# Sparse heads in pairs inside the common loop, output products between a turn and its values, a third place for the last output chunk

## The chip, the cores and the metric

The kernel runs on one core of one Trainium2 chip. The metric is device time in microseconds (us); smaller is better. TensorE (PE) multiplies, VectorE (DVE) and ScalarE (ACT) work on tiles, GpSimd (POOL) takes some elementwise work, SyncE (SP) only starts DMAs. Each engine works through its own queue in order and waits there for semaphores.

## The reference, cut to what matters

The program is two transformer layers and one further block on 256 tokens of width 1024, in float32. The change lies in the first layer's mixer. Its output is a product of 16 heads (1024 columns) with a 1024x1024 matrix. Eight heads (NSA) have a compressed, a selected and a window branch; with 256 tokens the last two are full causal attention on two sets of keys. Eight heads (DSA, "sparse") attend to the 64 best tokens by an index score, with keys and values made from a latent of 128 numbers per token:

```python
ckv = rms_norm(kv_lat, kv_norm)
q_lat = jnp.einsum('bshd,rhd->bshr', q, w_uk)
_, idx = lax.top_k(isc, topk)                 # isc: index score, topk = 64
logits = jnp.einsum('bqhr,bqkr->bhqk', qlb, c_sel) * scale + bias
p = masked_softmax(logits, (dist >= 0)[:, None])
o_lat = jnp.einsum('bhqk,bqkr->bqhr', p, c_sel)
o = jnp.einsum('bqhr,rhd->bqhd', o_lat, w_uv)
```

The kernel does not gather: it adds -1e30 to the logits of tokens that are not chosen. Then come the output product, a residual with layer norm, and the MLP.

## The kernel before, in words

Weights stream from memory in 1 MB chunks into a ring of four slots. Each chunk is split into a rounded high part (ACT, `round_weights`, L493) and a remainder (DVE, `lower_weights`, L499). The split parts have two places in SBUF for chunks 0 to 11 and three from chunk 12 (the first MLP chunk, MLP0) on; a place can be rewritten when the chunk before it there is "used" by PE. Chunks 8 to 11 (EV_OUT to EV_OUT + 3) hold the output matrix. A split product is three matmuls (L505 to L507).

Attention works in units of 384 columns (the two query tiles see 128 and 256 keys). Units 0 to 15 are NSA heads by branch, units 16 to 23 (DSA0 to DSA0 + 7) the sparse heads. For each unit: PE makes logits; DVE scales them, adds the bias and takes two maxima (`unit_logits_vector`, L1056 to L1061); ACT takes exponentials (L1067); DVE makes the coefficient (L1328, L1330, for sparse units L1325); POOL scales by it (L1074); PE turns the result with three transposes (L1082); ACT copies it out of PSUM (`pT`, L1089); PE multiplies with the values. There are four slots (NB) for units. In units 2 to 14 DVE also finds the chosen tokens in eight rounds (L1311, L1316); their mask is made at unit 14.

The first loop takes NSA units in pairs, d = 0 to 7: two units' logits lie in the two halves of the rows of the PE array, and their values in the two halves of its columns (L1046, L1048, L1175, L1177). It also makes the sparse queries in the latent space (`ql`, L1205). After it sparse units go one by one over the full array: logits against the latent (L1038, L1039), values (L1236, L1237), an ACT copy `olat`, and a product with `w_uv` (L1247). Chunk 8 and chunk 9 of the output product (`out_step`, 24 matmuls each) lie after pair 6's values and in step 3; chunks 10 and 11 come in a tail of 48 matmuls (`out_tail`), after DVE has finished head pair 7. Then `norm_vector` and `norm_scalar` run, and the MLP starts.

PSUM has eight banks. `Banks.take` (L184) pops the first free bank and makes PE wait until whatever was there last has been read; a bank taken with hold stays out of the list until `give`. The output product holds four banks from `out_begin` on. A finished head pair's bank is given back at once, but whoever takes it next waits for DVE's `head_out_vector` (L1097), which comes after ACT's `head_out_scalar` (L1093).

Of the kernel before, what the change touches and what calls it, by code (L numbers as in the profile page):

```python
# [291 lines left out]
def program(nc, I, out):  # L292
    ctx = ExitStack()
    with ctx:
# [69 lines left out]
        qlatT = mem.take("qlatT", 8, SEQ, at=iq_at)  # L364
# [16 lines left out]
        ukT = mem.take("ukT", 4, P)  # L381
# [10 lines left out]
        olat = mem.take("olat", 2, SEQ, at=ln_at + 4 * UC)  # L392
# [615 lines left out]
        def ev_gpsimd(e):  # L1008
# [16 lines left out]
            e.wait_ge(*landed.at("bias", 2))  # L1025
# [8 lines left out]

        def unit_logits_tensor(e, u, lhs, rhs):

            b = ps.take(e, ("unit", u), vec, "z", u)
            e.matmul(b[:, 0:P], lhs(0), rhs(tok(0)), start=True, stop=True)  # L1038
            e.matmul(b[:, P:UC], lhs(1), rhs(ALL), start=True, stop=True).then_inc(*pe.up("logits", u))  # L1039
# [67 lines left out]
        def out_multiply(e, tag, c, src, t, first, last):  # L1107
            w_ = weights(c)
            for kk, (h_, l_) in enumerate(src):
# [42 lines left out]
        def sparse_logits_tensor(e, h):  # L1152
            unit_logits_tensor(e, DSA0 + h, lambda t: qlatT[:, h, tok(t)], lambda c: ckvT[:, c])

        def two_logits_tensor(e, d):
            h, branch = NSA[2 * d]
            kk = BRANCH[branch][0]
            pair_logits_tensor(e, 2 * d, lambda r, t: qT[HALVES[r], h // 2, tok(t)], lambda r, c: kk[HALVES[r], h // 4, c])

        def two_values_tensor(e, d):  # L1160
            h, branch = NSA[2 * d]
            g, c0, i = h // 4, BRANCH[branch][1], h // 2
            v_ = lambda t: v_sw[:, t, c0 + g * HALF:c0 + (g + 1) * HALF]
            if branch == 0:
                ps.take(e, ("heads", i), vec, "o", "nsa", i, hold=True)
                if d == 0:
                    e.wait_ge(*act.at("pcT"))
                for r in range(2):
                    base = 32 * ((h + r) % 4)
                    e.matmul(ps.of(("heads", i))[HALVES[r], 0:SEQ], v_cmp[base:base + NCMP, g, :],  # L1170
                             pcT[base:base + NCMP, g, :], start=True, stop=False)
            b = ps.of(("heads", i))
            for r in range(2):
                e.wait_ge(*act.at("pT", 2 * d + r))
                e.matmul(b[HALVES[r], 0:SEQ], v_(0), pT_of(2 * d + r)[:, 0:SEQ], start=False, stop=False)  # L1175
            for r in range(2):
                m = e.matmul(b[HALVES[r], P:SEQ], v_(1), pT_of(2 * d + r)[:, SEQ:UC], start=False, stop=branch == 1)  # L1177
                m.then_inc(*pe.up("values", 2 * d + r))
            if branch:
                pe.also("heads", i)  # L1180
                ps.give(("heads", i))

        def attention_tensor(e):
            for d in range(8):
                two_logits_tensor(e, d)
# [4 lines left out]
                elif d < 3:  # L1190
# [5 lines left out]
                    if d == 2:  # L1196
                        pe.also("used", 7)
                elif d < 7:
                    js = (2 * d - 6, 2 * d - 5)
                    for j in js:  # L1200
                        ps.take(e, ("ql", j), act, "ql", j)
                    if d == 3:
                        e.wait_ge(*act.at("dq1", 1))
                    for j in js:
                        e.matmul(ps.of(("ql", j))[:, 0:SEQ], ukT[HALVES[j % 2], j // 2, :], dqT[HALVES[j % 2], j // 2, :],  # L1205
                                 start=True, stop=True).then_inc(*pe.up("ql", j))
# [4 lines left out]
            e.wait_ge(*act.at("ql", 7))  # L1211
            sparse_logits_tensor(e, 0)
            unit_turn_tensor(e, 13, pool)
            sparse_logits_tensor(e, 1)
            two_values_tensor(e, 6)
            out_begin(e, "y0")
            e.wait_ge(*vec.at("o", "nsa", 1))
            out_step(e, "y0", EV_OUT, heads_of(0), True)
            for r in range(2):
                unit_turn_tensor(e, 14 + r, pool)  # L1220
            for step in range(2, 8 + 4):
                if step < 8:
                    sparse_logits_tensor(e, step)
                if step == 2:
                    two_values_tensor(e, 7)
                h = step - 2
                if 0 <= h < 8:
                    unit_turn_tensor(e, DSA0 + h, pool)
                if step == 3:
                    e.wait_ge(*vec.at("o", "nsa", 3))  # L1230
                    out_step(e, "y0", EV_OUT + 1, heads_of(1), False)
                h = step - 3
                if 0 <= h < 8:
                    b, p_ = ps.take(e, ("olat", h), act, "olat", h), pT_of(DSA0 + h)
                    e.wait_ge(*act.at("pT", DSA0 + h))
                    e.matmul(b[:, 0:SEQ], ckv[:, 0, :], p_[:, 0:SEQ], start=True, stop=False)  # L1236
                    e.matmul(b[:, P:SEQ], ckv[:, 1, :], p_[:, SEQ:UC], start=False, stop=True).then_inc(  # L1237
                        *pe.up("values", DSA0 + h))
                h = step - 4
                if h >= 0:  # L1240
                    pair = ("heads", 4 + h // 2)
                    if h % 2 == 0:
                        ps.take(e, pair, vec, "o", "dsa", 4 + h // 2, hold=True)
                        if h == 0:
                            e.wait_ge(*landed.at("w_uv"))
                    e.wait_ge(*act.at("olat", h))
                    e.matmul(ps.of(pair)[HALVES[h % 2], 0:SEQ], w_uv[:, h * HALF:(h + 1) * HALF], olat[:, h % 2, :],  # L1247
                             start=True, stop=True).then_inc(*pe.up("project", h))
                    if h % 2:
                        pe.also(*pair)  # L1250
                        ps.give(pair)
            ada_sum(e, 0, 9)
            e.wait_ge(*vec.at("o", "dsa", 7))
            out_tail(e, "y0", (EV_OUT + 2, EV_OUT + 3), (heads_of(2), heads_of(3)))

        def attention_scalar(e):
# [3 lines left out]
            for d in range(8):  # L1260
                if d >= 2:
                    turn_copy(2 * d - 3)
                unit_logits_scalar(e, 2 * d)
                if d < 2:
                    round_weights(e, 7 + d)
                elif 3 <= d < 7:
                    for j in (2 * d - 6, 2 * d - 5):
                        e.wait_ge(*pe.at("ql", j))
                        e.activation(qlatT[:, j, :], ps.of(("ql", j))[:, 0:SEQ], ACT.Copy).then_inc(*act.up("ql", j))
                if d >= 1:  # L1270
# [5 lines left out]
                unit_logits_scalar(e, 2 * d + 1)  # L1276
                if d == 0:
                    pair_copy(e, dqT, "dq0", 0)
                if d >= 3 and d % 2:
                    head_out_scalar(e, (d - 3) // 2, ("heads", (d - 3) // 2), "nsa")  # L1280
            turn_copy(13)
# [1788 lines left out]
```

## Time and profile before

| | |
|---|---|
| median of 3 runs | 1225.04 us (1224.74 to 1226.72) |
| profiled execution | 1224.25 us, span 1222.4 us, mean granted clock 0.973 |
| busy: PE, DVE, ACT, POOL | 1124.7, 803.6, 610.8, 65.0 us |
| chain that ended last, by engine | PE 73%, DVE 15%, ACT 7%, DMA 2% |
| attention stage | about 139.8 to 218.4 us |
| output tail and layer norm | 218.4 to 239.7 us, then the MLP |

A row of the timeline is: start us, duration us, engine, line, operation, output<-input, shape and count, and in brackets how long the engine had been idle and what ended that. A row of the windows is: stretch, length, busy us (count) of PE, PEld, DVE, ACT and POOL, mean granted clock (1.00 is 2.4 GHz), DMA share, GB/s. Durations overlap a little in the pipelines, so the distance between two starts is what an instruction costs its queue.

### The profile page before, as it was taken

The page shows a single profiled execution, that of the slowest core. Times are in us where ns is not written, and L with a number is a line of the kernel's source. Part 1 is how long each engine was busy: PE and PEld are TensorE (multiplying, and loading weights), DVE is VectorE, ACT ScalarE, POOL GpSimd, SP SyncE. Part 2 cuts the span into 40 slices and gives each one's busy share as a digit, 9 for nine tenths or more (in the row PEclk, how much of TensorE's full clock was granted, in tenths as well). Part 3 has the DMA queues.
Part 4 walks back from the last instruction along what each step waited for, and adds up shares of the span by engine and source line. Part 5 has one row for each costly group of instructions (what it writes and reads, how often), then busy time and mean ns, then how long its engine had stood idle before and what let it go on. Part 6 is the DMA issues. An engine that isn't in the chain of part 4 may idle for free.

```text
span 1222.4 us, 20615 instructions
## 1 busy us (share of the span) xinstructions
PE 1124.7 (92%) x8503; PEld 1004.6 (82%) x8503; DVE 803.6 (66%) x1288; ACT 610.8 (50%) x1097; POOL 65.0 (5%) x85
## 2 busy tenths in 40 slices
PE   1788988999999989989999999999779998999997
PEld 1666956899899889878899998999668887999996
DVE  7676795779998686657846446766766656444443
ACT  0441466554444456665554554546673427554543
POOL 0011176000000000000000000020000000000000
PEclk9989999999999999989999999989887999999999
DMA  9678711389999545433775653160000043655540
GB/s 368 265 297 317 263 36 69 109 301 352 363 337 348 206 145 181 155 105 110 284 278 176 233 176 106 70 228 14 1 2 20 2 142 117 210 202 174 198 147 35
DMA packets 33277, 218.31 MB, mean 179 GB/s; under 512 B 4496, under 2 KB 5264, under 8 KB 8480
## 3 DMA queue, kind: packets, MB, share of 16 engines
q1 hardware_dynamic: 33184, 217.00, 49.1%
q8 instruction: 68, 1.11, 0.4%
q14 instruction: 25, 0.20, 0.1%
HBM read 215.93 MB, written 1.05 MB: 177 GB/s over the span
## 4 chain that ended last, share of the span: by engine, by line
PE 73%; DVE 15%; ACT 7%; DMA 2%; issue 1%; POOL 0%; SPq 0%; DVEq 0%; ACTq 0%
PE bank L505 20%; PE bank L507 20%; PE bank L506 20%; DVE low L499 2%; DVE ada_acc L574 2%; PE bank L530 1%; DMA ring<-ada_halves 1%; DVE act_low L1451 1%; ACT high L493 1%; PE bank L587 1%; PE bank L2301 1%; PE bank L2303 1%; PE bank L2289 1%; DVE y_tmp L1496 1%; DVE y_tmp L1503 1%
## 5 line engine op out<-in xcount | busy, mean ns | idle before, releaser
L499 DVE TENSOR_TENSOR low<-ring,high 128x2048 fp32r<-128x2048 f32 (+1 forms) x139 | 317.9, 2289 | 253.4 <-ACT high L493 253.0
L493 ACT ACTIVATE high<-ring 128x2048 fp32r<-128x2048 f32 (+1 forms) x139 | 264.5, 1905 | 258.6 <-PE bank L507 184.7
L505 PE MATMUL bank<-act_high,high 128*128 128x256 f32 (+1 forms) x1112 | 321.2, 289 | 6.0 <-DVE act_low L1451 6.0
L507 PE MATMUL bank<-act_high,low 128*128 128x256 f32 (+1 forms) x1112 | 315.9, 284 | 0.0
L506 PE MATMUL bank<-act_low,high 128*128 128x256 f32 (+1 forms) x1112 | 315.8, 284 | 0.0
L505 PE MATMUL bank<-high,act_high 128*128 128x512 f32 (+1 forms) x632 | 233.9, 370 | 3.8 <-DVE act_low L2829 1.8
L507 PE MATMUL bank<-high,act_low 128*128 128x512 f32 (+1 forms) x632 | 231.5, 366 | 0.0
L506 PE MATMUL bank<-low,act_high 128*128 128x512 f32 (+1 forms) x632 | 231.5, 366 | 0.0
L505 PEld LDWEIGHTS bank<-act_high,high 128*128 128x128 f32 x1112 | 213.5, 192 | 11.2 <-DVE act_low L1451 6.8
L506 PEld LDWEIGHTS bank<-act_low,high 128*128 128x128 f32 x1112 | 213.5, 192 | 2.7 <-issue 1.7
L507 PEld LDWEIGHTS bank<-act_high,low 128*128 128x128 f32 x1112 | 213.4, 192 | 0.0
L505 PEld LDWEIGHTS bank<-high,act_high 128*128 128x128 f32 x632 | 120.0, 190 | 24.6 <-DVE act_low L2829 2.0
L507 PEld LDWEIGHTS bank<-high,act_low 128*128 128x128 f32 x632 | 119.8, 190 | 20.5
L506 PEld LDWEIGHTS bank<-low,act_high 128*128 128x128 f32 x632 | 120.0, 190 | 17.7
L574 DVE SCALAR_TENSOR_TENSOR ada_acc<-ring,c_act,ada_acc 128x512 f32<-128x512 f32 x168 | 126.5, 753 | 7.7 <-DMA ring<-ada_halves 0.2
L545 PE MATMUL bank<-cols 128*128 128x128 f32 x446 | 54.1, 280 | 0.0
L1067 ACT ACTIVATE zb<-zb,ust 128x128 f32<-128x128 f32 x80 | 35.8, 448 | 36.7 <-DVE ust L1061 35.7
L545 PEld LDWEIGHTS bank<-cols 128*128 128x128 f32 x446 | 52.9, 197 | 0.3
L587 PE MATMUL bank<-ones,ada_acc 128*128 128x1 f32 x128 | 19.0, 270 | 26.3 <-DVE ada_acc L574 26.3
L1074 POOL TENSOR_SCALAR zb<-zb,ust 128x128 f32<-128x128 f32 (+1 forms) x48 | 40.3, 852 | 47.3 <-DVE ust L1330 38.2
L587 PEld LDWEIGHTS bank<-ones,ada_acc 128*128 128x128 f32 x128 | 19.4, 225 | 27.6 <-DVE ada_acc L574 14.2
L2198 POOL MEMSET conv<- 128x24 f32 x1 | 0.1, 127 | 553.3 <-DVE x_tok L1980 553.3
(479 smaller groups left out, 1347.1 us busy)
## 6 DMA issues: line engine op xcount, KB each, us to landing
ring<-chunks SPq DMA_DIRECT2D x138, 1024.0 KB, 5.1
ring<-ada_halves SPq DMA_DIRECT2D x48, 1024.0 KB, 6.4
ring<-raw_cmp SPq DMA_DIRECT2D x4, 1024.0 KB, 7.0
gate_rows<-ada_b SPq DMA_DIRECT2D x4, 512.0 KB, 7.1
bias<-bias_by_distance SPq DMA_DIRECT2D x1, 2048.0 KB, 11.9
ln_rows<-ln_g SPq DMA_DIRECT2D x4, 512.0 KB, 5.0
ln_rows<-ln_b SPq DMA_DIRECT2D x4, 512.0 KB, 6.2
hT<-xT SPq DMA_DIRECT2D x1, 1024.0 KB, 8.4
```

The lines of the kernel that those rows point to most:

```text
L493: e.activation(weights(c)[0], in_ring(("w", c)), ACT.Copy).then_inc(*act.up("high", c))
L499: e.tensor_tensor(low, in_ring(("w", c)), high.bitcast(F32), ALU.subtract).then_inc(*vec.up("low", c))
L505: e.matmul(out_, ah, bh, start=start, stop=False)
L506: e.matmul(out_, ah, bl, start=False, stop=False)
L507: return e.matmul(out_, al, bh, start=False, stop=stop)
L530: last = e.matmul(out_, src[:, k, toks], w[:, k, c0:c0 + n_cols], start=k == 0, stop=k == n - 1)
L545: m = e.matmul(b[:, 0:P], ident, ident, start=True, stop=True)
L574: e.scalar_tensor_tensor(acc, w_[:, k, :], c_, acc, ALU.mult, ALU.add).then_inc(*vec.up())
L587: m = e.matmul(b[:, i:i + 1], acc[:, i * P:(i + 1) * P], ones[:, 0:1], start=True, stop=True)
L1067: x = e.activation(z[:, c], z[:, c], ACT.Exp, bias=st[:, t:t + 1], accum_out=st[:, 2 + t:3 + t])
L1074: x = e.tensor_scalar(z[:, c], z[:, c], st[:, 4 + t:5 + t], None, ALU.mult)
L1451: e.tensor_tensor(halves_[1][grp], dst[grp], halves_[0][grp].bitcast(F32), ALU.subtract).then_inc(*vec.up("h", tag, t, i))
```

## The change

It does these things:

- Keys (`kdT`) and values (`vd`) of the sparse heads are made in full from the latent: two takes of two 256-column products (`sparse_keys_tensor`) and two 512-column products (`sparse_values_tensor`), with four ACT copies of 512 columns. They replace the eight `ql` products, their eight copies, the eight `olat` copies and the eight products with `w_uv`.
- Sparse units run as pairs 8 to 11 of the common loop, in the same halves of the array as the NSA pairs.
- Output products of chunks 8, 9 and the first token tile of 10 stand in iterations 8 to 12, 12 matmuls each, between the turn of unit 2d - 3 and the values of pair d - 2. The tail keeps 36 of its 48 matmuls, 6 of them before the wait for head pair 7.
- Chunk 9 is split in the loop: ACT at the end of iteration 4, DVE after unit 9. Chunks 10 and 11 follow at iterations 10 and 11 on ACT, after unit 22 and after unit 23 on DVE.
- The sum for part 9 of the modulation (`ada_sum(0, 9)`) moves from the end of the stage to iteration 4 on PE, and its DVE read (`ada_put`) to after unit 11.
- Three places hold from chunk 11 on instead of from chunk 12.
- One load of 256 KB (`ukT`) becomes another of the same size (`w_uk`), on the same queue at the same point, and POOL's first bias read waits for one load instead of two.

```diff
-            may = range(2 if c < MLP0 or IN2 + 9 <= c < MLP2 else 3)
+            may = range(2 if c < MLP0 - 1 or IN2 + 9 <= c < MLP2 else 3)
@@ attention_tensor
-            for d in range(8):
-                two_logits_tensor(e, d)
+            for d in range(DOUBLES + 2):
+                if d < DOUBLES:
+                    two_logits_tensor(e, d)
                 if d >= 2:
                     unit_turn_tensor(e, 2 * d - 3, pool)
...
+                elif d < 5:
+                    sparse_keys_tensor(e, d - 3)
                 elif d < 7:
-                    (ql products)
+                    sparse_values_tensor(e, d - 5)
+                if d == 4:
+                    ada_sum(e, 0, 9)
+                if d == 8:
+                    out_begin(e, "y0")
+                    e.wait_ge(*vec.at("o", "nsa", 1))
+                    e.wait_ge(*low_made(EV_OUT))
+                if 8 <= d < 10:
+                    m = out_multiply(e, "y0", EV_OUT, heads_of(0), d - 8, True, False)
...
+                if 10 <= d < 12:
+                    m = out_multiply(e, "y0", EV_OUT + 1, heads_of(1), d - 10, False, False)
...
+                if d == 12:
+                    e.wait_ge(*vec.at("o", "dsa", 5))
+                    e.wait_ge(*low_made(EV_OUT + 2))
+                    out_multiply(e, "y0", EV_OUT + 2, heads_of(2), 0, False, False)
                 if d >= 2:
                     two_values_tensor(e, d - 2)
-                if d >= 1:
+                if 1 <= d <= DOUBLES:
                     unit_turn_tensor(e, 2 * d - 2, pool)
...
+            out_multiply(e, "y0", EV_OUT + 2, heads_of(2), 1, False, False, (0,))
+            e.wait_ge(*low_made(EV_OUT + 3))
             e.wait_ge(*vec.at("o", "dsa", 7))
-            out_tail(e, "y0", (EV_OUT + 2, EV_OUT + 3), (heads_of(2), heads_of(3)))
+            out_multiply(e, "y0", EV_OUT + 3, heads_of(3), 0, False, True).then_inc(*pe.up("out", "y0", 0))
+            out_multiply(e, "y0", EV_OUT + 2, heads_of(2), 1, False, False, (1,)).then_inc(*pe.up("used", EV_OUT + 2))
+            out_multiply(e, "y0", EV_OUT + 3, heads_of(3), 1, False, True).then_inc(*pe.up("out", "y0", 1))
@@ attention_scalar
+                if d >= 10:
+                    head_out_scalar(e, d - 6, ("heads", d - 6), "dsa")
+                if d == 4:
+                    round_weights(e, EV_OUT + 1)
+                if d == 10:
+                    round_weights(e, EV_OUT + 2)
+                if d == 11:
+                    round_weights(e, EV_OUT + 3)
@@ attention_vector
+                if u == 11:
+                    ada_put(e, 0, 9)
...
+                if u >= DSA0:
+                    mask_bias(u - DSA0 + 2)
...
+                if u == 9:
+                    lower_weights(e, EV_OUT + 1)
+                if u in (21, 23):
+                    head_out_vector(e, 4 + (u - 21) // 2, ("heads", 4 + (u - 21) // 2), "dsa")
+                if u == 22:
+                    lower_weights(e, EV_OUT + 2)
+            coefficient(DSA0 + 7)
+            lower_weights(e, EV_OUT + 3)
+            for i in (6, 7):
+                head_out_vector(e, i, ("heads", i), "dsa")
             lower_weights(e, MLP0)
```

## Rows read from the trace of the kernel before

**Rows 1.** Windows: first loop's second half, and sparse units up to head pair 7

```profile
167.97:182.90 14.93, 12.63 (x90) 7.17 (x89) 13.26 (x58) 10.67 (x39) 11.80 (x16) 1.00 0.01 2
182.90:218.38 35.48, 32.34 (x171) 23.71 (x168) 20.21 (x57) 21.96 (x59) 19.95 (x25) 1.00 0.20 65
```

**Rows 2.** Timeline of DVE: first instruction of units 9, 10 and 16

```profile
166.20 0.28 DVE L1056 SCALAR_TENSOR_TENSOR zb<-bank,bias 128x128 f32<-128x128 f32 x1
...
167.97 0.28 DVE L1056 SCALAR_TENSOR_TENSOR zb<-bank,bias 128x128 f32<-128x128 f32 x1
...
182.90 0.28 DVE L1056 SCALAR_TENSOR_TENSOR zb<-bank,dbias 128x128 f32<-128x128 f32 x1
```

**Rows 3.** Timelines of ACT and DVE: exponentials of unit 9, then chunk 9's split

```profile
167.36 0.40 ACT L1067 ACTIVATE zb<-zb,ust 128x128 f32<-128x128 f32 x1
...
168.26 0.47 ACT L1089 ACTIVATE pT<-bank 128x384 f32<-128x384 f32 x1
...
186.48 1.90 ACT L493 ACTIVATE high<-ring 128x2048 fp32r<-128x2048 f32 x1
...
188.41 2.55 DVE L499 TENSOR_TENSOR low<-ring,high 128x2048 fp32r<-128x2048 f32 x1 [1.64 <-ACT high L493]
```

**Rows 4.** Timeline of PE: branch start, pair values, turn, pair logits, turn

```profile
154.97 0.65 PE L1170 MATMUL bank<-pcT,v_cmp 15*64 15x256 f32 x4
155.55 0.65 PE L1175 MATMUL bank<-pT,v_sw 128*64 128x256 f32 x4
...
156.35 0.55 PE L1082 MATMUL bank<-cols,zb 128*128 128x128 f32 x3
156.83 0.49 PE L1046 MATMUL bank<-k_win,qT 64*128 64x128 f32 x4
...
157.68 0.55 PE L1082 MATMUL bank<-cols,zb 128*128 128x128 f32 x3
```

**Rows 5.** Timeline of PE: a sparse unit's values, product with w_uv, logits, turn

```profile
203.57 0.60 PE L1236 MATMUL bank<-pT,ckv 128*128 128x256 f32 x2
...
204.32 0.65 PE L1247 MATMUL bank<-olat,w_uv 128*64 128x256 f32 x2
204.90 0.49 PE L1038 MATMUL bank<-ckvT,qlatT 128*128 128x128 f32 x2
...
205.65 0.50 PE L1082 MATMUL bank<-cols,zb 128*128 128x128 f32 x3
```

**Rows 6.** Timelines of ACT and DVE: the two copies of head pair 2

```profile
181.76 0.36 ACT L1093 ACTIVATE act_high<-bank 128x256 fp32r<-128x256 f32 x1
...
182.16 0.42 DVE L1097 TENSOR_TENSOR act_low<-bank,act_high 128x256 fp32r<-128x256 f32 x1 [0.72 <-ACT act_high L1093]
```

**Rows 7.** Timelines of PE and DVE: the output tail and the start of the norm

```profile
218.44 0.50 PE L505 MATMUL bank<-high,act_high 128*128 128x512 f32 x1
...
229.57 1.06 PE L1418 MATMUL bank<-cols,n_tok 128*128 128x128 f32 x8
...
219.76 2.29 DVE L499 TENSOR_TENSOR low<-ring,high 128x2048 fp32r<-128x2048 f32 x1 [1.07 <-ACT high L493]
...
223.57 1.37 DVE L1496 TENSOR_TENSOR y_tmp<-bank,gate_rows 128x512 f32<-128x512 f32 x2 [0.71 <-PE bank L507]
...
229.08 1.31 DVE L1496 TENSOR_TENSOR y_tmp<-bank,gate_rows 128x512 f32<-128x512 f32 x2
```

**Rows 8.** Timeline of PE and windows: an idle stretch of PE, and the granted clock

```profile
90.50 0.39 PE L657 MATMUL bank<-cols,hid 30*128 30x30 f32 x2 [4.86 <-DVE hid L882]
...
88.00:92.00 4.00, 0.92 (x4) 0.59 (x5) 3.93 (x4) 2.14 (x6) 0.00 (x0) 0.50 1.01 428
...
208.00:212.00 4.00, 2.59 (x16) 1.76 (x15) 1.66 (x7) 2.86 (x12) 2.43 (x4) 1.00 0.00 0
```

**Rows 9.** Timelines of PE and ACT: chunk 99's last product, chunk 101's rounding

```profile
834.94 0.28 PE L507 MATMUL bank<-high,act_low 128*128 128x256 f32 x1
...
835.59 1.90 ACT L493 ACTIVATE high<-ring 128x2048 fp32r<-128x2048 f32 x1
```

More of the change, by code:

```diff
@@ L363, in program @@
         raw = mem.take("raw", 4, SEQ)
-        qlatT = mem.take("qlatT", 8, SEQ, at=iq_at)
+        kdT = mem.take("kdT", 4, SEQ, at=iq_at)
+        vd = mem.take("vd", QT, 512, at=iq_at + 4 * SEQ)
         k_sel = mem.take("k_sel", 2, SEQ)
@@ L380, in program @@
         pcT = mem.take("pcT", 2, SEQ)
-        ukT = mem.take("ukT", 4, P)
+        w_uk = mem.take("w_uk", 512)
         NB = 4
@@ L1033, in program @@
         st_of = lambda u: ust[:, u % NB, :]
[L1035 to L1039, printed above, removed]
         def pair_logits_tensor(e, u, lhs, rhs):
@@ L1105, in out_begin, with out_multiply @@
                     ps.take(e, (tag, t, half), vec, "y", tag, t, half, hold=True)
-        def out_multiply(e, tag, c, src, t, first, last):
+        def out_multiply(e, tag, c, src, t, first, last, kks=range(KW)):
             w_ = weights(c)
-            for kk, (h_, l_) in enumerate(src):
+            for kk in kks:
+                h_, l_ = src[kk]
                 for half in range(2):
@@ L1160, in two_values_tensor @@
         def two_values_tensor(e, d):
[L1161 to L1171, printed above, removed]
+            if d >= N_NSA:
+                i = d - N_NSA + 4
+                first, last, stage = True, True, "dsa"
+                v_ = lambda r, t: vd[:, t, (2 * (i - 4) + r) * HALF:(2 * (i - 4) + r + 1) * HALF]
+                ps.take(e, ("heads", i), vec, "o", "dsa", i, hold=True)
+                if i == 4:
+                    e.wait_ge(*act.at("vd", 1))
+            else:
+                h, branch = NSA[2 * d]
+                g, c0, i = h // 4, BRANCH[branch][1], h // 2
+                first, last = False, branch == 1
+                v_ = lambda r, t: v_sw[:, t, c0 + g * HALF:c0 + (g + 1) * HALF]
+                if branch == 0:
+                    ps.take(e, ("heads", i), vec, "o", "nsa", i, hold=True)
+                    if d == 0:
+                        e.wait_ge(*act.at("pcT"))
+                    for r in range(2):
+                        base = 32 * ((h + r) % 4)
+                        e.matmul(ps.of(("heads", i))[HALVES[r], 0:SEQ], v_cmp[base:base + NCMP, g, :],
+                                 pcT[base:base + NCMP, g, :], start=True, stop=False)
             b = ps.of(("heads", i))
@@ L1210, in attention_tensor @@
                     unit_turn_tensor(e, 2 * d - 2, pool)
[L1211 to L1251, printed above, removed]
@@ L1344, in sparse_logits_vector @@
                                    slot_free(DSA0 + h, pe, "turn"))
-            for u in range(len(NSA)):
-                h = NSA[u][0]
-                unit_logits_vector(e, u, SCALE, bias[:, h, P:SEQ], bias[:, h, :], slot_free(u, pe, "turn"))
+            for u in range(DSA0 + 8):
+                if u < DSA0:
+                    h = NSA[u][0]
+                    unit_logits_vector(e, u, SCALE, bias[:, h, P:SEQ], bias[:, h, :], slot_free(u, pe, "turn"))
+                else:
+                    sparse_logits_vector(u - DSA0)
                 if u == 2:
```

133 lines of the change are left out of this document (55 added, 78 removed).

## The prediction

> **What bounds the kernel now.** I read the chain that ended last first: it runs along PE almost everywhere, so a stage with PE busy throughout is set by PE. The attention stage is not one of them, so I then read the windows, and then the timelines of the four engines side by side. In the second half of the first loop DVE is busy 13.26 of 14.93 us [rows 1]: units 10 to 15 go at the pace of DVE, which does logits, maxima and the search for the chosen tokens, while PE has slack. From unit 16 on the picture turns: DVE is busy 20.21 of 35.48 us and PE 32.34 [rows 1]. There PE does the full-array sparse units and the output products, and DVE and ACT wait. So work added to DVE or a wait of DVE before unit 16 costs its full length; after it, work taken from PE pays. Then come a tail of 48 matmuls and the norm on DVE [rows 7].
>
> **Chunk 9 in the first loop.** Its split costs DVE 2.3 us (the row here shows 2.55, the same form stands at 2.29 in the tail) [rows 3, 7]. Before it lay at 186.5 to 191 us, under PE's output products of chunk 8, and cost nothing. Now DVE meets it after unit 9. It can start only when ACT has rounded, and ACT rounds after the exponentials of unit 9: these take 0.90 us of ACT's queue (167.36 to 168.26), and the rounding 1.90 [rows 3]. ACT starts unit 9 about when DVE finishes that unit's maxima; DVE has some 0.7 us of its own left (unit 9's search step, unit 8's coefficient; a unit takes 1.77 us from 166.20 to 167.97, of which 1.05 are logits and maxima) [rows 2]. So DVE waits 0.90 + 1.90 + 0.1 - 0.7 = 2.2 us and then works 2.2 to 2.3 us. Behind it in DVE's queue stand the logits of unit 10, so exponentials, POOL's scaling and the turns wait too. Unit 10 starts at 167.97 + 4.45 = 172.4 us. No one catches up before unit 16, since DVE is the bound there: unit 16 starts at 182.90 + 4.45 = 187.4. Bounds: 2.3 (no wait) to 5.0; I take 4.45, the sum of the rows.
>
> **Keys, values, the moved sum.** In the first loop `ql` goes and four products come. The trace shows no 512-column product of this kind; 384 columns cost 0.75 us (204.90 to 205.65) [rows 5], so 512 lie between 0.75 and 1.0 us, four in total 3.4 us against some 2.5 for `ql`. ACT copies of 512 columns take the place of twice as many of 256. PE and ACT have slack there: nothing, -0.2 to +0.5 us. The moved `ada_sum` costs about 1 us of PE there and frees it in front of the tail, where it is on the path: -1 us, part of the walk below. It takes a bank at iteration 4; counting takes through `Banks.take`, seven others follow, and the eighth is the first bank for the logits of pair 6. That bank is free only after `ada_put`, which DVE reaches after unit 11, now at 176.2 us. PE stands before it from its last turn, near 172.0. Queued behind are the turn of unit 9, `vd` and pair 4's values. DVE wants unit 12 at about 177, so by itself this costs 0.2 us. Its second effect is below, under the clock.
>
> **From unit 16 to head pair 7.** Per pair PE before needs two units of 0.75 values + 0.58 product + 0.75 logits [rows 5] = 4.16 us, now 0.80 values (155.55 to 156.35) + 0.85 logits (156.83 to 157.68) = 1.65 [rows 4]: 10 us of PE work less in four pairs. But the order changes too, so I walk through it. Prices: turn 0.48 (156.35 to 156.83), 12 output matmuls 11.13 x 12 / 48 = 2.78 [rows 4, 7]. An iteration with all parts is 0.85 + 0.48 + 2.78 + 0.80 + 0.48 = 5.4 us. The output products start when the fourth held bank is free; counting takes, it was head pair 2's, so they start after DVE's copy of it, at 187.6 us. Iteration 8 then needs 2.78 + 0.58 + 0.80 + 0.48: 192.3. Iteration 9: 197.7. In iteration 10 the turn of unit 17 takes the bank of head pair 3, since with four banks held only four circulate, for five takes per iteration. That bank waits for a chain that begins with the last turn of iteration 9, which now comes after the output products: ACT's copy 0.37, the exponentials 0.90 [rows 3], the head copy 0.36, DVE's copy 0.42 [rows 6], handovers 0.2: 2.25 us, against 0.85 us of PE logits meanwhile. PE waits 1.4 us, and again in iteration 11: 197.7 + 2 x (5.4 + 1.4) = 211.3. In iteration 12 the product waits openly for head pair 5, by the same chain 2.0 us: 211.3 + 0.3 (turn) + 2.0 + 2.78 + 0.80 + 0.48 = 217.7. Iteration 13 has a turn, a wait of about 1.1 us for ACT's copy of it, and values 0.80: near 219.9; two copies, 0.78 + handovers: head pair 7 is ready at 220.8 instead of 218.38 us. So of 10 us only 2.0 come through (35.5 us before from unit 16 on, 33.4 now). Bounds: 0 to -5 (without the bank waits).
>
> **Tail and norm.** PE has 30 matmuls behind that point instead of 48, 4.2 us less. But DVE must first lower MLP0's chunk, which waits for ACT's rounding behind its last head copy: it starts 1.38 us after head pair 7 (218.38 to 219.76) and takes 2.29, the modulation 0.8 more [rows 7]. DVE is free 4.5 us after head pair 7, where before the norm began 5.2 after (223.57), having waited 0.71 for PE [rows 7]. So of 4.2 us 0.7 arrive, and 0.1 to 0.3 at the second token tile (229.08): -0.9. The second tile starts at 220.8 + 9.75 = 230.6: +1.5 us against 229.08. Bounds of the tail -0.7 to -2.5. The rest, norm and MLP, keeps its length.
>
> **Places and loads.** Chunk 11 goes to the third place and MLP0 to the second, both free long before. Far off, chunk 101 now waits for chunk 99 instead of 98: its rounding starts at 835.59 and chunk 99's last product ended at 835.22 [rows 9], 0.4 us to spare, so 0; at worst 0.5. SP is moved past nothing; its chunk 13 may go earlier, chunk 16 starts 2 us later but is the fifth chunk of the MLP. 0.
>
> **The clock.** Around the bank wait PE has, from 168.9 to 176.4 us, one pair's values and one turn, 1.3 us of work in 7.5, and nothing in the last 4.4. The trace shows such a stretch: PE idle 4.86 us before 90.50; the granted clock was 0.50 from 88 to 92 [rows 8]. It shows too that 2.59 us busy in 4 keeps 1.00 [rows 8]. So I expect the 1.2 GHz level for some 3 to 7 us, of which 2.4 to 4.9 fall behind 176.4, when PE has logits of pair 6, a turn, `vd`, values, a turn and logits of pair 7 back to back, and DVE waits for those logits. Half of that stretch is lost, 1.2 to 2.4 us; I take 1.7. It can be 0 if the wait turns out shorter, and a second low stretch adds 1.7. The Trainium skill (TensorE: Matmul & The Clock Gate, section on HAM oscillation) says that a matmul burst after a long enough idle gap starts at the half clock; it speaks against this change. By it the sum is +3.2 us; if the chip took the stretch as it took 208 to 212, the sum would be +1.5.
>
> **Sum.** 4.45 (chunk 9) - 2.05 (units 16 to head pair 7, 35.5 less 33.4) - 0.9 (tail) = +1.5 us, and +1.7 by the clock: +3.2. The profiled execution took 1224.25 us, 0.8 below the median of 1225.04; 1224.25 + 3.2 = 1227.45 there, 1228.2 against the median.
>
> **The rivals.** First, the bubble without the clock: the same walk, but PE's quiet stretch is short or broken, as it would be if `ada_put` came early. For it: the first loop has many gaps of PE and keeps 1.00. Against it: 1.3 us of work in 7.5. It gives +1.5: 1226.5. Second, faster: chunk 9's wait and work are absorbed. That holds if what follows unit 16 isn't set by when DVE gets there but by PE's own queue. Then 4.45 drops out, and -2.05 - 0.9 remain: 1222.1. For it: PE is busy 32.34 of 35.48 us there and loses 10 us of work. Against it: DVE has only 1.7 us of slack in the 14.93 us that follow [rows 1]. It decides from where PE, not DVE, is late at unit 16. Third, worse: a second low stretch of clock, or a longer chain through the banks, at another 1.7 to 2.5 us: 1230.4. That the pairs don't run side by side is excluded by the rows of the NSA pairs of the same shape [rows 4].
>
> **How the numbers follow.** Forecast 0.50 (its own range 1227.2 to 1229.8), no clock 0.28, absorbed 0.14, worse 0.08. A measurement of this kernel can tell about 0.2%, 2.45 us, from no change. Slower: 0.08 and 0.46 of the forecast's 0.50 = 0.54; the other 0.04 lie within; same: 0.28 + 0.04 = 0.32; faster 0.14. The range reaches down past the no-clock case into the absorbed one and up to the worse one: 1223.0 to 1230.8 leaves out about a tenth on each side.
>
> **What would show it.** In the changed profile: chunk 9's remainder on DVE near 170 us with an idle time of about 2.2 us before it; unit 10 near 172.4 and unit 16 near 187.4; PE idle over 4 us before pair 6's logits, then a granted clock near 0.5 to 0.7 over the next 4 us; turns of units 17 and 19 idle about 1.4 us, released by DVE's head copies; head pair 7 near 221 to 222.5; the norm's first DVE instruction 4.5 us later, with no wait for PE. The prediction is wrong if unit 16 starts before 185, if the bank waits are missing, or if the clock stays at 1.00.

## The result and the profile after

The change makes the kernel slower: a median of 1234.42 us (1234.3 to 1234.93, 4 runs) against 1225.78 us (1224.74 to 1226.72), a ratio of 1.0065 with a 95% interval of 1.0045 to 1.0085. The ratio is the recorded one; the two medians divided give 1.0070. The forecast was 1228.2, with a range up to 1230.8: the sign was right, +3.2 us was not, it is +8.6. Two kernels further below, put_early and chunk9_late, each had one execution at a far lower clock (1598 and 1837 us), which their medians leave out.

| | before | after |
|---|---|---|
| span of the profiled execution | 1222.4 us | 1232.5 us |
| mean granted clock | 0.973 | 0.968 |
| unit 0 (DVE) to the MLP's first matmul, "the stage" | 99.07 us | 105.79 us |
| granted clock in the stage | 1.00 | 0.94 |

Of the 10.1 us between the two spans 6.7 lie in the stage. Of the rest, 6.25 us come before it and -2.9 behind it, in code that the change leaves alone. These two vary between executions whatever the kernel: in the 14 profiled ones of this study the stage begins at 140.4 to 147.2 us, and 979.8 to 983.2 us lie behind it. The later begin is the clock too: from 100 us to the begin of the stage it is 0.96 on average before and 0.85 after, and PE is busy 6.3 us longer with the same code (38.51 and 44.81 us). So I compare stages, and medians.

Windows of after, columns as in [rows 1]: the first two answer to them (units 10 to 16, unit 16 to head pair 7), then the stage, and three short stretches inside it.

```profile
178.63:195.50 16.87, 10.69 (x61) 5.61 (x61) 13.54 (x59) 9.97 (x34) 9.95 (x14) 0.80 0.19 64
195.50:232.25 36.75, 31.66 (x170) 21.49 (x171) 17.28 (x56) 17.34 (x51) 20.06 (x25) 0.91 0.17 58
...
146.92:252.71 105.79, 86.99 (x554) 62.90 (x555) 73.78 (x238) 59.55 (x165) 45.52 (x56) 0.94 0.21 70
...
180.00:187.00 7.00, 4.34 (x15) 2.17 (x17) 5.59 (x28) 4.38 (x17) 3.84 (x6) 0.51 0.33 133
197.20:200.40 3.20, 3.20 (x10) 2.06 (x10) 1.22 (x6) 0.46 (x2) 3.20 (x5) 0.50 0.00 0
224.40:227.80 3.40, 3.40 (x9) 2.31 (x7) 2.29 (x1) 0.66 (x2) 0.61 (x1) 0.50 0.04 12
```

In [rows 1] both windows had the clock at 1.00. Now three stretches stand at the 1.2 GHz level, and the second window is longer than before, although PE and DVE are busy for less of it.

Timeline of DVE, after: unit 9, chunk 9's remainder, unit 10, the read of the moved sum, unit 16 (they answer to [rows 2, 3]); then the lowering of MLP0, the norm's first step and its second tile [rows 7].

```profile
172.44 0.28 DVE L1050 SCALAR_TENSOR_TENSOR zb<-bank,bias 128x128 f32<-128x128 f32 x1
...
176.43 2.29 DVE L499 TENSOR_TENSOR low<-ring,high 128x2048 fp32r<-128x2048 f32 x1 [2.13 <-ACT high L493]
...
178.63 0.28 DVE L1050 SCALAR_TENSOR_TENSOR zb<-bank,bias 128x128 f32<-128x128 f32 x1
...
182.45 0.15 DVE L601 TENSOR_TENSOR ada_cols<-bank,cols 128x4 f32<-128x4 f32 x1
...
195.50 0.28 DVE L1050 SCALAR_TENSOR_TENSOR zb<-bank,dbias 128x128 f32<-128x128 f32 x1
...
233.64 2.29 DVE L499 TENSOR_TENSOR low<-ring,high 128x2048 fp32r<-128x2048 f32 x1 [1.38 <-ACT high L493]
...
236.66 1.28 DVE L1488 TENSOR_TENSOR y_tmp<-bank,gate_rows 128x512 f32<-128x512 f32 x2
...
242.07 1.28 DVE L1488 TENSOR_TENSOR y_tmp<-bank,gate_rows 128x512 f32<-128x512 f32 x2
```

DVE waits 2.13 us for ACT's rounding and works 2.29: unit 10 comes 6.19 us behind unit 9 instead of 1.77.

Timeline of PE, after: logits of pair 6, `vd`, the first output product (12 matmuls to the values at 200.33), the turns of units 17 and 19, the product of iteration 12 and the values behind it.

```profile
182.66 0.80 PE L1040 MATMUL bank<-k_sel,qT 64*128 64x128 f32 x4 [4.49 <-DVE ada_cols L601]
...
184.93 1.91 PE L1207 MATMUL bank<-w_uv,ckvT 128*128 128x512 f32 x2
...
195.94 0.47 PE L505 MATMUL bank<-high,act_high 128*128 128x512 f32 x1 [2.24 <-DVE zb L1050]
...
200.33 0.71 PE L1180 MATMUL bank<-pcT,v_cmp 15*64 15x256 f32 x4
...
209.87 0.55 PE L1076 MATMUL bank<-cols,zb 128*128 128x128 f32 x3 [1.32 <-DVE act_low L1091]
...
216.62 0.55 PE L1076 MATMUL bank<-cols,zb 128*128 128x128 f32 x3 [1.32 <-DVE act_low L1091]
...
223.39 0.50 PE L505 MATMUL bank<-high,act_high 128*128 128x512 f32 x1 [1.64 <-DVE act_low L1091]
...
227.93 0.65 PE L1185 MATMUL bank<-pT,vd 128*64 128x256 f32 x4
```

Four of these five waits are those of the prediction, at their places. The fifth, 2.24 us before the first output product, lies in its walk but isn't named there. (The profile puts its end down to DVE's L1050; the instruction right ahead of that one in DVE's queue is the copy of head pair 2, for which PE waits by the count of the takes.) What the prediction had not is behind two of the waits: the output products of iterations 8 and 12 take 4.39 and 4.54 us (195.94 to 200.33, 223.39 to 227.93) where 12 such matmuls were priced at 2.78. The stretches 197.2 to 200.4 and 224.4 to 227.8 are these. The 12 matmuls behind each of the two waits of 1.32 us kept the full clock: they take 2.93 and 2.94 us (210.17 to 213.10, 216.93 to 219.87).

### The profile page after: what moved, and what is told of

Read it like the earlier page. It is cut to its first block, busy times and chain, and to the rows that moved or that the text cites. A ratio compares the mean times of both kernels' runs of the same rounds, so it can differ in the third digit from the quotient of the medians.

```text
span 1232.5 us, 20555 instructions
## 1 busy us (share of the span) xinstructions
PE 1124.5 (91%) x8483; PEld 1002.2 (81%) x8483; DVE 802.8 (65%) x1288; ACT 607.7 (49%) x1085; POOL 64.3 (5%) x85
## 4 chain that ended last, share of the span: by engine, by line
PE 72%; DVE 16%; ACT 7%; DMA 2%; issue 2%; POOL 0%; SPq 0%; DVEq 0%; ACTq 0%
PE bank L505 19%; PE bank L507 19%; PE bank L506 19%; DVE ada_acc L574 2%; DVE low L499 2%; PE bank L530 2%; ACT high L493 1%; DMA ring<-ada_halves 1%; DVE act_low L1443 1%; PE bank L2293 1%; PE bank L587 1%; PE bank L2295 1%; ACT hT L1423 1%; PE bank L2281 1%; PE bank L1076 1%
```

## The experiments

All of them in one table: distances in us from the profiled execution of each, the stage being their sum and the 25.5 us from unit 0 to unit 9 that all have; the clock is that from unit 10 to 16 and from 16 to head pair 7. Head pair 7 is the end of DVE's last head copy. Ratios are as recorded, against the kernel before on the same chip, whose median was 1225.71 us for the first four of the experiments, 1226.09 for filled, heads_early, chunk9_early and reordered, and 1225.69 for the other four. Each distance comes from one execution, and each median from 4 to 10.

| kernel | 9 to 10 | 10 to 16 | 16 to head pair 7 | to the MLP | stage | clock | median, ratio [95%] |
|---|---|---|---|---|---|---|---|
| before | 1.77 | 14.93 | 35.48 | 21.36 | 99.07 | 1.00, 1.00 | 1225.78 |
| after | 6.19 | 16.87 | 36.75 | 20.46 | 105.79 | 0.80, 0.91 | 1234.42, 1.0065 [1.0045, 1.0085] |
| before_new_inputs | 1.78 | 14.93 | 35.47 | 21.33 | 99.03 | 1.00, 1.00 | 1226.88, 1.0002 [0.9986, 1.0018] |
| after_old_inputs | 6.20 | 19.08 | 36.77 | 20.47 | 108.04 | 0.73, 0.91 | 1235.34, 1.0063 [1.0046, 1.0079] |
| put_early | 6.20 | 16.35 | 36.80 | 20.46 | 105.34 | 0.79, 0.91 | 1232.28, 1.0047 [1.0029, 1.0066] |
| chunk9_late | 1.77 | 18.09 | 39.44 | 20.46 | 105.29 | 0.81, 0.87 | 1231.73, 1.0035 [1.002, 1.0049] |
| filled | 6.19 | 14.92 | 33.63 | 20.46 | 100.73 | 1.00, 1.00 | 1226.97, 1.0004 [0.9992, 1.0016] |
| filled_first | 6.19 | 14.93 | 35.20 | 20.46 | 102.30 | 1.00, 0.95 | 1228.25, 1.0012 [0.9995, 1.0028] |
| chunk9_early | 6.20 | 16.76 | 35.46 | 21.32 | 105.26 | 0.69, 1.00 | 1233.56, 1.0058 [1.0037, 1.0079] |
| chunk9_early_filled | 6.20 | 14.93 | 35.46 | 21.36 | 103.45 | 1.00, 1.00 | 1230.52, 1.0031 [1.0013, 1.0049] |
| chunk9_at_17 | 1.78 | 16.50 | 36.76 | 20.45 | 101.02 | 0.90, 0.91 | 1228.18, 1.0017 [0.9999, 1.0034] |
| heads_early | 6.20 | 16.60 | 31.71 | 21.02 | 101.06 | 0.79, 0.95 | 1228.44, 1.002 [1.0002, 1.0038] |
| reordered | 1.85 | 14.52 | 31.53 | 20.45 | 93.87 | 1.00, 0.95 | 1219.57, 0.9946 [0.9925, 0.9967] |
| reordered_filled | 1.84 | 14.53 | 30.11 | 20.91 | 92.92 | 1.00, 1.00 | 1219.36, 0.994 [0.9918, 0.9962] |

### The stretch ahead of the stage: the changed load

In the changed kernel's profile the stage began 6.2 us later, so the load itself was suspected. The first kernel is the changed one with the load read from an input at the old one's place, the second the kernel before with its load read from where the new one is.

```diff
-            e.dma_start(w_uk, I["dsa_w_uk"][0].rearrange("r h d -> r (h d)")).then_inc(*landed.up("w_uk"))
+            e.dma_start(w_uk.rearrange("p (a b) -> p a b", a=4), I["ukT"][:, :, :]).then_inc(*landed.up("w_uk"))
...
```

> The changed kernel, except that its new load of 256 KB comes from an input that stands where the old one stood, with the old one's name and shape; the instructions on the engines are the same. In the profile of the changed kernel the attention stage begins 6.2 us later than before, although nothing ahead of it was changed but this input. Theory A (the place of the input sets which DMA lands late, and PE's clock follows): the stage begins again near 139.7 us, and the time falls by about 6 us to 1228. Theory B (the delay comes from what the changed instructions do, or is there by chance): the stage begins near 146 us and the time stays at 1234.4, within 1 us.

> The kernel before, with its input for this load put where the changed kernel has its own. Theory A: the attention stage begins near 146 us and the time rises by about 6 us to 1232. Theory B: stage begin 139.7 us, time 1225.8 within 1 us.

Neither moved by the 6 us of theory A: 1235.34 and 1226.88 us (the second 1.1 to 1.2 above the kernel before, just past the 1 us that theory B allowed), and the stages began at 142.6 and 142.8 us, where neither theory had them. So the begin of the stage varies, and the load has no part in the 8.6 us. The first shows too that the stage of the same instructions is not always equally long: 108.04 us here, with unit 10 to 16 at 19.08 us and a clock of 0.73.

### One step back at a time: chunk 9, the moved sum

```diff
-                if d == 4:
+                if d == 8:
                     round_weights(e, EV_OUT + 1)
...
-                if u == 9:
+                if u == 17:
                     lower_weights(e, EV_OUT + 1)
```

and, by itself, `ada_put` behind unit 9 (`if u == 9` for `if u == 11`).

> The changed kernel with the split of output chunk 9 moved from the first loop (ACT iteration 4, DVE after unit 9) to iteration 8 on ACT and after unit 17 on DVE, where DVE waits for PE. My theory: 4.4 us of waiting and work leave DVE while DVE sets the pace, nothing comes back later, so the time falls by 4 to 5 us to about 1230; unit 10 starts 1.8 to 2.1 us after unit 9 instead of 6.2. Rival (the later loop is set by PE alone): unit 16 starts earlier but head pair 7 ends as late, 1233.5 to 1234.5.

> The changed kernel with the DVE read of modulation part 9 after unit 9 instead of unit 11, so that the bank for the logits of pair 6 is free and PE's idle 4.5 us before them are broken up. My theory: the granted clock stays at 1.00 or is low for less of the work behind 182 us, so 1 to 2 us less, 1232.4 to 1233.4. Rival (the bank wait costs nothing since DVE is the bound, and PE is quiet there anyway): 1234.4 within 0.5, with the clock low as before.

Both gave something, neither much: 1231.73 us for chunk9_late, between the two theories, and 1232.28 for put_early, a hair below the 1232.4 to 1233.4 of its first theory. With chunk 9 late, unit 10 is back at 1.77 us, but ACT now rounds so late that DVE waits 7.20 us for it behind unit 17. With the early `ada_put` the bank wait is gone, but PE, past pair 6's logits, stands 3.09 us before the next turn instead, since DVE is as late as before, and the clock falls all the same. In both it is at 0.8 and 0.9 of full speed. As an estimate from the windows' lengths and mean clocks, the time at half clock in the two is 13.4 us in after, 13.5 in put_early and 17 in chunk9_late: removing one wait moved the low stretches and did not lessen them. So put_early's own theory, a clock that recovers, did not come true, though its time did.

### The clock by itself

The direct test leaves order and waits as they are and only keeps PE occupied in them, with products of the identity that nobody reads, in a bank whose last reader is done:

```diff
+        def fill(e, u, n):
+            e.wait_ge(*act.at("pT", u))
+            idle_products(e, ps.of(("turn", u)), n)
...
+                if d in (10, 11):
+                    fill(e, 2 * d - 4, 5)
...
                 if d == 8:
+                    fill(e, 12, 9)
                     out_begin(e, "y0")
...
                 if d == 12:
+                    fill(e, 20, 5)
...
+                if d == 5:
+                    fill(e, 7, 18)
```

> The changed kernel with idle 128x128 products of the identity put into PE's waits in the loop, each group into a transpose bank whose copy ACT has already made: 18 behind the transposes of unit 8 (PE waits 4.49 us there), 9 ahead of the first output product (waits 2.24 us), 5 in iterations 10, 11 and 12 (wait 1.32, 1.32 and 1.64 us). Nothing else is changed and the result is the same. Theory C (the missing 5.4 us of my sum are TensorE's clock: granted 0.5 over 180.0-186.9, 197.1-200.5 and 224.4-227.8 of the changed kernel's span, the output products of iteration 12 4.39 and 4.54 us instead of 2.78): these stretches go, the output products come back to 2.8 us, from unit 16's start on DVE to head pair 7 it takes 33.3 to 34.5 us instead of 36.75, from unit 10 to 12 5.0 instead of 5.7 us, and the median is 1229 to 1231.5 us against 1234.4. Rival D (the loop's order is what costs it, the clock is beside the point): from unit 16 to head pair 7 stays within 0.5 us of 36.75 although the clock is full, and the median within 1 us of 1234.4. If the low stretches stay or only move, neither is told.

> The changed kernel with the first of the five groups of idle products alone: 18 behind the transposes of unit 8, in the wait of 4.49 us before pair 6's logits. Theory I (each low stretch has its own wait ahead of it): the stretch at 180-187 goes (unit 10 to 12 5.0 instead of 5.7 us, unit 12 to 16 10.0 instead of 11.2), those behind the first output product and in iteration 12 stay, from unit 16 to head pair 7 36.0 to 36.8 us; the median is 1231.5 to 1233.5. Rival J (the first low stretch brings the others): from unit 16 to head pair 7 33.5 to 34.5 us as with all five groups, the median 1226.5 to 1228.5.

Windows of filled, unit 10 to 16 and unit 16 to head pair 7, then PE's timeline (which counts two rows for each idle product; the first row is cut off at its start): the 18 idle products, the logits of pair 6, 9 idle products, the first output product and that of iteration 12 with its last row.

```profile
177.23:192.15 14.92, 14.09 (x111) 10.12 (x110) 13.53 (x59) 9.98 (x34) 9.96 (x14) 1.00 0.20 73
192.15:225.78 33.63, 32.76 (x202) 23.18 (x202) 17.27 (x56) 17.35 (x51) 20.05 (x25) 1.00 0.17 57
```

```profile
176.81 3.96 PE L551 MATMUL bank<-cols 128*128 128x128 f32 x34
181.25 0.49 PE L1040 MATMUL bank<-k_sel,qT 64*128 64x128 f32 x4 [0.47 <-DVE ada_cols L601]
...
190.19 2.17 PE L551 MATMUL bank<-cols 128*128 128x128 f32 x18
...
192.59 0.47 PE L505 MATMUL bank<-high,act_high 128*128 128x512 f32 x1 [0.23 <-DVE zb L1050]
...
218.51 0.50 PE L505 MATMUL bank<-high,act_high 128*128 128x512 f32 x1 [0.22 <-DVE act_low L1091]
...
221.14 0.39 PE L507 MATMUL bank<-high,act_low 128*128 128x512 f32 x1
```

The releasers are the same as in after, so PE is released by the same steps; but the clock is 1.00 throughout, the product of iteration 12 takes 2.95 us (218.51 to the values at 221.46) instead of 4.54, the first one 2.91 instead of 4.39, and 1.95 and 3.12 us go from the two windows. The median is 1226.97 us, which can't be told from the kernel before, and 7.4 us below the changed one, more than I expected (1229 to 1231.5). It isn't the one profile alone: the mean clock of a whole execution is 0.972 to 0.975 in all ten of filled, and 0.965 to 0.968 in all four of the changed kernel. So the clock is a cause, shown, and by the profiled stages the largest (5.06 us). With the first group alone the first window is back (14.93 us), the second goes only half way (35.20 us, against 36.0 to 36.8 and 33.5 to 34.5 by the two theories): the stretch behind the first output product is gone too, though its wait of 2.24 us is still there, and a low one remains at 214 to 217. So neither theory holds whole, and the median of 1228.25 us lies with the second (1226.5 to 1228.5). As far as one profile shows, the low stretches are tied to one another, not each to its own wait.

### The heads' bank

ACT's copy of a finished head pair is put ahead of the copy of the second turn and the second unit's exponentials, so that DVE's head copy, for which PE waits, can follow earlier.

```diff
+                    if d == 9:
+                        head_out_scalar(e, 3, ("heads", 3), "nsa")
+                    if d >= 10:
+                        head_out_scalar(e, d - 6, ("heads", d - 6), "dsa")
                     turn_copy(2 * d - 2)
...
-                if d >= 10:
+                if d == 13:
                     head_out_scalar(e, d - 6, ("heads", d - 6), "dsa")
```

> The changed kernel with one order changed on ACT: from iteration 9 on the copy of head pairs 3 to 6 out of their bank stands ahead of the copy of the second transposes and of the second unit's exponentials, instead of behind them. The bank of the head pair is then free for the next transposes some 1.3 us earlier. Theory E (the bank waits of iterations 10 to 12 are on the path): PE's waits on the low half of the heads (1.32, 1.32 and 1.64 us in iterations 10, 11 and 12) are gone or under 0.3 us, from unit 16 to head pair 7 it takes 1.5 to 4 us less than 36.75, and the median is 1230.5 to 1233 us. Rival F (DVE's and GpSimd's steps behind the logits are late next): the waits go but from unit 16 to head pair 7 it stays within 0.7 us of 36.75; the median stays at 1234 to 1235.

Windows of heads_early, unit 10 to 16 and unit 16 to head pair 7:

```profile
177.91:194.51 16.60, 10.44 (x61) 5.59 (x61) 13.53 (x59) 9.97 (x34) 9.95 (x14) 0.79 0.19 65
194.51:226.22 31.71, 29.78 (x170) 20.75 (x171) 17.34 (x56) 17.93 (x51) 18.26 (x25) 0.95 0.15 44
```

Theory E, and more than it: the waits on the low half of the heads are gone in iterations 10 and 11 and 0.36 us in 12 (where a turn now waits 0.79 us for a bank of logits), and 5.04 us go from unit 16 to head pair 7 (1.5 to 4 expected), to 1228.44 us (1230.5 to 1233 expected). The three waits were 4.3 us together and 1.15 are left, so 3.1 of the 5.04 are waits. The low stretch of iteration 12, worth 1.6 us in after, is gone too (the clock is 1.00 from 200 us on, and 0.95 instead of 0.91 over the window); the one behind the first output product is still there.

### Chunk 9 alone, with and without the clock

The kernel before, with only chunk 9's split early, and then PE's new waits filled with 13 idle products in the same manner.

```diff
+                if d == 4:
+                    round_weights(e, EV_OUT + 1)
...
-            round_weights(e, EV_OUT + 1)
...
+                if u == 9:
+                    lower_weights(e, EV_OUT + 1)
...
-            lower_weights(e, EV_OUT + 1)
```

> The kernel before with one part of the change alone: output chunk 9 is rounded by ACT at the end of iteration 4 and lowered by DVE behind unit 9 (which the third place allows it), and no longer between the loops. Nothing else moves. Theory G (the steps stand in DVE's queue ahead of unit 10): from unit 9 to unit 10 on DVE 6.2 instead of 1.77 us (+4.4), between the loops about 2.3 us less of DVE and 1.8 us less of ACT, so that head pair 7 comes 2 to 4.4 us later than in the kernel before, and the median is 1227.5 to 1231 us, if the clock doesn't fall in the stretch. If it does (granted 0.5 for 3.4 to 6.9 us behind the wait), 1229 to 1233. Rival H (the later stages take it up, and the +8.6 us of the change are all of its new loop for the sparse heads): head pair 7 within 1 us of the kernel before, the median within 1 us of 1225.8.

> The kernel before with chunk 9 early, and idle products in the waits of PE that this brings: 6 ahead of the values of pair 3 (waits 1.22 us), 5 behind the transposes of unit 8 (1.23 us), 2 ahead of those of unit 9 (1.05 us). Without them from unit 0 to the MLP took 105.3 us against 99.1 of the kernel before, 4.4 of it between unit 9 and 10 and 1.8 between 12 and 16, where the clock was 0.5 over 179.0-189.3. Theory G2 (4.4 us are DVE's wait and work, 1.8 the clock): unit 9 to 10 stays 6.2 us, unit 12 to 16 comes back from 11.9 to 10.1, the stage is 103.3 to 103.7 us and the median 1230 to 1232. Rival (the 1.8 us are queued work behind the late chunk): unit 12 to 16 stays over 11.5 us with a full clock, median 1233 to 1234.

Windows of chunk9_early: unit 10 to 16, unit 16 to head pair 7, the low stretch and the 5 us ahead of it. Then the first two windows of the filled one.

```profile
178.88:195.64 16.76, 14.35 (x73) 7.71 (x74) 13.35 (x58) 10.04 (x36) 10.35 (x14) 0.69 0.18 64
195.64:231.10 35.46, 32.33 (x171) 23.73 (x168) 17.66 (x56) 20.13 (x58) 17.85 (x25) 1.00 0.12 35
179.00:189.30 10.30, 8.61 (x39) 4.52 (x39) 7.87 (x37) 6.45 (x24) 6.00 (x8) 0.50 0.30 103
...
174.00:179.00 5.00, 3.07 (x18) 1.59 (x18) 2.84 (x7) 3.01 (x6) 1.50 (x2) 1.00 0.01 3
```

```profile
173.04:187.97 14.93, 11.72 (x83) 6.86 (x83) 13.27 (x59) 9.90 (x36) 10.36 (x14) 1.00 0.21 72
187.97:223.43 35.46, 32.33 (x171) 23.73 (x168) 17.67 (x56) 20.14 (x58) 17.84 (x25) 1.00 0.12 34
```

This one edit costs 6.2 us of the stage: 4.43 by DVE's wait and work, 1.83 by the clock, which the idle products give back exactly (14.93 us again). And the place that chunk 9 left gives nothing: 35.46 us from unit 16 to head pair 7 against 35.48, with 2.5 us less of DVE in it. There it had been hidden, as the prediction had it; my expectation here of up to 2.4 us was wrong, and the median of 1233.56 us lies just past the 1229 to 1233 expected with a low clock. With the idle products it is 1230.52 us (1230 to 1232 expected). The two profiled executions lie at the ends of their groups, 3.3 us above the one median and 3.3 below the other, and of the ten executions of the filled kernel five have a mean clock of 0.969 or 0.970 and five of 0.975 to 0.977: the split into 4.43 and 1.83 us is that of two profiles.

Its complement is the changed kernel with chunk 9 alone elsewhere, early enough on ACT this time (`d == 7`, `u == 17`).

> The changed kernel with chunk 9 alone put elsewhere: rounded by ACT at the end of iteration 7, lowered by DVE behind unit 17; the gate's column sum stays behind unit 11 and the copies of the head pairs where they were. The complement of chunk9_early. If chunk 9 is most of the +8.6 us: unit 9 to 10 1.8 us, unit 16 to head pair 7 33.5 to 37 us by where the clock falls, stage 96.5 to 101, median 1221 to 1227. If the new loop itself is slower than the two loops were: unit 9 to 10 1.8 us, but the stage 102 us or more and the median over 1228.

The stage is 101.02 us, at the upper end of the one theory, and the median 1228.18, just inside the other. The 4.4 us are gone; the bank wait before pair 6's logits is 1.70 instead of 4.49 us, and both windows are as long as in after (16.50 and 36.76), with the clock at 0.90 and 0.91. So without chunk 9's step in the first loop the new stage is 2 us longer than the old one (by the medians 2.5 us, with an interval that just reaches no change), and it is so with a low clock.

### All of it together

Reordered: `ada_put` behind unit 9, chunk 9 at `d == 7` and `u == 17`, the heads' copies early. Then the same with `fill(e, 12, 9)` ahead of the first output product.

> The changed kernel with four of its steps put elsewhere: the gate's column sum is added behind unit 9 instead of 11, chunk 9 is rounded by ACT at the end of iteration 7 instead of 4, and lowered by DVE behind unit 17 instead of 9 (in an earlier run both at iteration 8 and later gave back the 4.4 us at unit 10, but put 2.7 us between unit 16 and head pair 7), and the copies of head pairs 3 to 6 stand earlier on ACT. By my sum for the change: unit 10 comes 1.77 us behind unit 9, no bank wait at pair 6's logits, no bank wait on the heads: stage from unit 0 to the MLP 95 to 98 us against 99.1 of the kernel before with a full clock, a median of 1221.5 to 1224.5. If the clock falls twice in it all the same (as in the two runs with a step moved), 101 to 104 us and 1226.5 to 1230.

> The reordered kernel (1219.57 us) with 9 idle products in PE's wait of 2.23 us before the first output product, behind which the clock was 0.5 over 185.7-189.1. From unit 16 to head pair 7 30.5 to 31.2 instead of 31.53 us, the median 1218.2 to 1219.6. If the idle products stand in the way of the first output product it is over 1220.

Windows of reordered, unit 10 to 16 and unit 16 to head pair 7; then unit 16 to head pair 7 of reordered_filled, and a stretch in its norm.

```profile
171.00:185.52 14.52, 11.00 (x75) 5.67 (x74) 13.28 (x60) 10.46 (x37) 11.29 (x16) 1.00 0.00 2
185.52:217.05 31.53, 29.61 (x170) 20.76 (x171) 20.20 (x57) 19.61 (x52) 20.29 (x25) 0.95 0.23 77
```

```profile
185.02:215.13 30.11, 28.38 (x172) 19.68 (x172) 20.58 (x57) 19.63 (x52) 20.36 (x25) 1.00 0.25 79
226.50:229.90 3.40, 3.40 (x19) 3.40 (x18) 2.70 (x6) 3.08 (x11) 0.00 (x0) 0.50 0.02 5
```

1219.57 us, ratio 0.9946 [0.9925, 0.9967]: faster than both kernels, with the same computation, and better than I expected (stage 95 to 98, 1221.5 to 1224.5 us). The parts add up where that can be tested: 36.76 us from unit 16 to head pair 7 (chunk9_at_17) less 5.04 (heads_early against after) is 31.72, measured 31.53. The first window gains 1.98 us (16.50 to 14.52), mostly by its clock (0.90 to 1.00). The idle products take another 1.42 us from unit 16 on and the low stretch comes back in the norm, 226.5 to 229.9; the median stays (1219.36).

## Why the prediction was wrong in size, step by step

- **Chunk 9 in the first loop** (+4.45; wait 2.2, work 2.2 to 2.3). Right: 2.13 and 2.29 us, unit 10 later by 4.42. Nothing was caught up before unit 16 (14.93 us at full clock in chunk9_early_filled, 14.93 before), and its old place had cost nothing (35.46 us from unit 16 to head pair 7 in chunk9_early, 35.48 before). The rival that the step is absorbed falls.
- **Keys, values, moved sum** (0, with a bank wait of PE of over 4 us that costs 0.2 directly). Right: 4.49 us, released by `ada_put`, and nothing lost as long as the clock is full.
- **Unit 16 to head pair 7** (33.4 us). Right at full clock: 33.63 in filled. The bank waits are 1.32 twice (1.4 predicted) and 1.64 us (2.0), ended by DVE's head copy. In the changed kernel itself it is 36.75.
- **Tail and norm** (-0.9; norm 4.5 us behind head pair 7, no wait for PE). Right: 4.41 us (232.25 to 236.66), and the part up to the MLP 20.46 instead of 21.36 us.
- **The clock** (+1.7). Here the sum failed. The term priced one low stretch, and the profile has three, which cost 5.07 us (1.95 + 3.12) where it stood at 1.7. For the first, 1.2 to 2.4 us was right: 1.95. The term put at nothing was the clock behind the later waits: the 2.24 us before the first output product, and those of 1.3 to 1.6 us that the walk had itself computed. Dense work stands behind each of the four, 12 matmuls of 512 columns. Behind two of them it ran mostly at half clock and took 1.5 and 1.6 us more (4.39 against 2.91 in filled, 4.54 against 2.95); behind the two of 1.32 us it did not. These are the 3.12 us that filled gives back from unit 16 on. A second low stretch had 0.08 of the chance and 1.7 to 2.5 us; it came with a third.
- **The sum.** Without the clock I had +1.5 us and 1226.5; filled has a stage longer by 1.66 us and a median of 1226.97. With it: 4.42 - 1.85 - 0.90 + 1.95 + 3.12 = 6.7 us in the profiled stage. The median is 8.6 higher, and where its other 1.9 us lie is open. The stage of the same instructions came out 2.25 us longer in another execution (after_old_inputs), so the two are not at odds, but which of the runs had how much was not measured.

What stays open is why the clock falls just where it does. The runs show that it falls and that idle products prevent it in this stage; they don't give a rule from which the place could be told.

## What to carry to other kernels

Once a new order has been walked through, list every wait of PE in it, also those that cost nothing, and look at what PE does next: where dense matmuls follow, price them at the low clock as well, at each wait, as the upper end of the range. Here three of five waits had a low stretch behind them, and with the first one filled only one of the other four. Occupying PE with idle products in a bank that nobody reads separates the two causes in one run; but the better cure is to remove the waits, since here the three for DVE's head copies were 4.3 us, and one ACT copy put ahead of another unit's exponentials left 1.15 of them. And a split that lies under another engine's long stretch is free only there: of the 6.2 us that chunk 9's step costs, 4.4 are its own time and wait in a queue that had no room.

## What the runs showed of the hardware

The clock fell without a long idle time. In chunk9_early no wait of PE around the place is over 1.23 us; it was busy for 3.07 us of the 5 ahead of 179.0, and then had the 1.2 GHz level for 10.3 us although it was busy for 8.61 of them. In chunk9_early_filled a wait of 1.44 us (before 176.16) is left and the clock stays at 1.00, so the length of one wait doesn't tell it either. I had taken 2.59 us busy in 4 as proof of safety [rows 8]; it is none. The Trainium skill (TensorE: Matmul & The Clock Gate, the section on a second failure mode, psum-queue depth-cycling) says that short pauses of PE between groups of matmuls, brought by cycling through the banks, are enough to make the clock swing. This trace agrees that short pauses suffice (1.21, 1.22 and 1.23 us, ended at 174.11, 177.06 and 179.63, with the clock at 1.00 until 179.0 and then at 0.50); that the cycling brought them it doesn't show, since the first two are ended by DVE's coefficient and by ACT's copy of a turn.

The same instructions also got different clocks: the changed kernel's window from unit 10 to 16 took 16.87 us at 0.80 and 19.08 us at 0.73. The two differ only in the input from which one load comes. So single profiles of such a kernel can't be trusted to better than some 2 us where the clock is low.
